# Four half vectors of the conditioning on VectorE from the query groups on, and one on TensorE

## The reference, cut to what matters

```
silu_c = silu(c);  silu_cc = silu(c_ctx)
for l in 0, 1:                                   # 2 layers, 256 tokens, width 2048
    sh_m, sc_m, gt_m, sh_f, sc_f, gt_f = split(silu_c @ w_mod[l] + b_mod[l], 6)
    ux = rmsnorm(x) * g[0] * (1 + sc_m) + sh_m
    if l == 0:
        k_c, v_c = split(modulate(ctx, ..., silu_cc) @ w_in[:, 2048:])
        f, q, k, v = split_even(ux @ w_in)       # 1024, 1024, 256, 256 columns
        attn = window_attention(rope(q), rope(k), v, k_c, v_c, sink)
        mix = concat([fft2 per group(f).real, attn]) @ w_out
    else:
        mix = short_conv_mix(ux, ...)
    x = x + gt_m * rmsnorm(mix)
    x = x + gt_f * rmsnorm(relu(modulate(x, g[2], sh_f, sc_f) @ w1)**2 @ w2)
```

## Time and profile before

| | us |
|---|---|
| median of three runs (2260.5 to 2265.11) | 2263.23 |
| profiled execution | 2260.15 |
| its span, first to last instruction | 2258.4 |
| TensorE busy in it | 2197.8 (97%) |
| VectorE busy | 1653.4 (73%) |
| ScalarE busy | 1019.5 (45%) |

### The profile page before, as it was taken

The page is one execution under the profiler, slowest core; times in us unless marked ns, Lnnn a source line. Parts: engine busy times, 40 slices in busy tenths (PEclk is TensorE's granted clock), DMA queues, the critical chain, the costliest instruction groups (busy, mean ns, idle before and its releaser), DMA issues.

```text
span 2258.4 us, 30977 instructions
## 1 busy us (share of the span) xinstructions
PE 2197.8 (97%) x11355; PEld 1806.4 (80%) x11355; DVE 1653.4 (73%) x1784; ACT 1019.5 (45%) x1269; POOL 97.7 (4%) x32
## 2 busy tenths in 40 slices
PE   6899999999999999999989999999999999999998
PEld 3478568788888888888868888887888888888887
DVE  0266767888788888888988889988888554654665
ACT  3163544554344345344454444446534443443443
POOL 0000000001010010110101101100011000000000
PEclk8899999999999999999999999999999999999999
DMA  9966978688888888889868788896887656666664
GB/s 374 352 224 226 373 273 298 231 295 278 302 275 285 290 272 292 294 275 318 291 213 279 272 298 280 275 310 226 288 286 247 198 193 189 188 193 193 205 195 149
DMA packets 253896, 592.63 MB, mean 262 GB/s; under 512 B 18082, under 2 KB 18610, under 8 KB 253234
## 3 DMA queue, kind: packets, MB, share of 16 engines
q1 hardware_dynamic: 253746, 590.63, 77.6%
HBM read 588.46 MB, written 2.10 MB: 261 GB/s over the span
## 4 chain that ended last, share of the span: by engine, by line
PE 87%; DVE 5%; DMA 4%; issue 2%; ACT 2%; SPq 1%; DVEq 0%; ACTq 0%
PE ps L520 30%; PE ps L526 15%; PE ps L595 11%; PE ps L596 11%; PE ps L597 11%; PE ps L559 2%; DMA early<-in_w_mod_dram 2%; DVE wlo L1276 1%; DMA mraw<-in_w_mod_dram 1%; DMA raw<-in_mlp_w_dram 1%; DVE acc L1286 1%; PE ps L481 1%; ACT whi L908 1%; DMA raw<-in_att_w_out_dram 1%; PE ps L687 0%
## 5 line engine op out<-in xcount | busy, mean ns | idle before, releaser
L1276 DVE TENSOR_TENSOR wlo<-raw,whi 128x1024 fp32r<-128x1024 f32 x712 | 901.0, 1270 | 429.1 <-ACT whi L908 427.7
L908 ACT ACTIVATE whi<-raw 128x1024 fp32r<-128x1024 f32 x712 | 751.7, 1059 | 946.9 <-PE ps L597 384.6
L520 PE MATMUL ps<-u,whi 128*128 128x512 f32 x2944 | 930.1, 397 | 9.8 <-DVE wlo L1276 5.7
L526 PEld LDWEIGHTS ps<-u,wlo 128*128 128x128 f32 x2944 | 555.1, 189 | 131.5
L526 PE MATMUL ps<-u,wlo 128*128 128x256 f32 x2944 | 580.2, 279 | 0.0
L595 PE MATMUL ps<-whi,h 128*128 128x512 f32 x1216 | 474.6, 390 | 6.9 <-DVE wlo L1276 6.8
L597 PE MATMUL ps<-whi,h 128*128 128x512 f32 x1216 | 473.2, 389 | 0.0
L596 PE MATMUL ps<-wlo,h 128*128 128x512 f32 x1216 | 473.2, 389 | 0.0
L520 PEld LDWEIGHTS ps<-u,whi 128*128 128x128 f32 x2944 | 450.2, 189 | 17.1 <-issue 10.8
L1286 DVE SCALAR_TENSOR_TENSOR acc<-mraw,cs,acc 128x1024 f32<-128x1024 f32 x240 | 306.7, 1278 | 3.9 <-DMA mraw<-in_w_mod_dram 3.9
L595 PEld LDWEIGHTS ps<-whi,h 128*128 128x128 f32 x1216 | 228.3, 188 | 57.3 <-DVE wlo L1276 10.2
(11 more groups left out here) (195 smaller groups left out, 1258.3 us busy)
## 6 DMA issues: line engine op xcount, KB each, us to landing
raw<-in_mlp_w_dram SPq DMA_DIRECT2D x512, 512.0 KB, 4.7
mraw<-in_w_mod_dram SPq DMA_DIRECT2D x272, 512.0 KB, 5.4
early<-in_w_mod_dram SPq DMA_DIRECT2D x96, 512.0 KB, 6.7
raw<-in_conv_w_in_dram SPq DMA_DIRECT2D x96, 512.0 KB, 5.2
raw<-in_att_w_in_dram SPq DMA_DIRECT2D x40, 512.0 KB, 4.4
raw<-in_att_w_out_dram SPq DMA_DIRECT2D x32, 512.0 KB, 6.4
raw<-in_conv_w_out_dram SPq DMA_DIRECT2D x32, 512.0 KB, 6.0
raw<-in_w_mod_dram SPq DMA_DIRECT2D x16, 512.0 KB, 7.1
```

Source lines behind the costliest of these rows:

```text
L520: return pe.matmul(ps[:, 4 * slot + m, :], whi[:, s % SLOTS, cols], src[:, k, :], start=(k == 0), stop=False)
L526: return pe.matmul(ps[:, 4 * slot + m, 0:T], wlo[:, s % SLOTS, cols], src[:, k, 0:T], start=False, stop=(k == KC - 1))
L908: act.activation(whi[:, s, :], raw[:, s, :], ACT.Copy).then_inc(hi_ready, 1)
L1276: dve.tensor_tensor(wlo[:, s, :], raw[:, s, :], whi[:, s, :], ALU.subtract).then_inc(lo_ready, 1)
```

## The change

Units 0, 1, 4 and 2, in this order, are summed on VectorE by `mraw`, in the accumulators 1, 0, 1, 0 (`FIRST_UNITS`, `FIRST_ACC`), and unit 3 alone on TensorE. That is 64 unit slabs on VectorE, as against 32 by `mraw` and 16 by `early`, and 16 on TensorE in place of 32; 80 loads in both. The late unit and its loads are gone. `UNITS_BESIDE` says how many unit slabs stand beside each weight slab: 6 beside 8 to 15, 9 beside 16 to 23, 4 each beside 24, 25 and 26, 28 beside 27 to 43 (steps t = 0 to 16) and 9 in steps 17 to 21. SyncE loads slab m+2 four weight slabs further on. TensorE's pairs are at t = 8 to 15. Columns are made for unit 0 ahead of the Fourier steps, unit 1 at t = 4, unit 2 at t = 22, in bank 2, after all 64 unit slabs; one gate is spread at t = 18, the other with output slab 1, after `finish_first(2, 2)`. The accumulator of the first two units is started anew once its columns are done (`columns_done`). The number of `mraw` buffers is the same.

```diff
@@ SyncE
-            for w in range(SL, W_F + 6):
-                att_slab(w)
-                for m in FIRST_LOADS.get(w, ()):
-                    first_unit_slab(m)
-            for t in range(-1, 17):
-                att_slab(W_F + t + 7)
-                ...
-                if t != 1 and t < 16:
-                    mix_pair(t if t > 0 else t + 1)
-                if t >= 0:
-                    first_unit_slab(t + 13)
-            ...
+            for w in range(SL, slab_of(PG_WO) + SL):
                 att_slab(w)
+                for m in units_beside(w - SLOTS):
+                    if m + 2 < len(FIRST_UNITS) * UNIT:
+                        first_unit_slab(m + 2)
+                if w == W_F + 6:
                     sp.wait_ge(slab_used, W_KV + SL)
+                for n in MIX_LOADS.get(w - (W_F + 7), ()):
+                    mix_pair(n)
+            for m in range(units_before(slab_of(PG_WO) + SLOTS) + 2, len(FIRST_UNITS) * UNIT):
+                first_unit_slab(m)
@@ TensorE
+            unit_columns(0, 6)
             for t in range(24):
                 ...
-                if t == 21:
-                    pe.wait_ge(mix_copied, 2)
-                    pe.wait_ge(m_used, UNIT)
+                if t == 4:
+                    unit_columns(1, 6)
+                if t == 18:
+                    pe.wait_ge(mix_copied, 1)
+                    pe.wait_ge(m_used, 3 * UNIT)
+                    spread_gate(ones, acc[:, 1, :], 6)
                 if t == 22:
-                    pe.wait_ge(m_used, DVE_FIRST * UNIT)
-                if t >= 21:
-                    unit_columns(t - 21)
+                    pe.wait_ge(pt_copied, 2 * HEADS)
+                    unit_columns(2, 2)
@@ VectorE
                     lo(SL * (i + 1) + s, s % SLOTS)
-                    for m in FIRST_SLABS[i][s]:
+                    for m in units_beside(SL * (i + 1) + s):
                         first_unit_slab(m)
@@
             for s in range(3):
                 lo(W_F + s, s)
-                first_unit_slab(8 + s)
+                for m in units_beside(W_F + s):
+                    first_unit_slab(m)
@@
-                if t < 21:
-                    first_unit_slab(11 + t)
+                for m in units_beside(W_F + 3 + t):
+                    first_unit_slab(m)
+                if t == 6:
+                    finish_first(0, 6)
+                    finish_first(1, 6)
                 ...
-                for k in LATE_AT.get(t, ()):
-                    late_unit_slab(k)
-            finish_first()
+            finish_first(2, 2)
@@ tables
-FIRST_SLABS = (((), (), (), (), (0,), (), (), (1,)), ((2,), (3,), (4,), (5,), (6,), (), (), (7,)))
+MIX_LOADS = {4: (0,), 6: (1,), 8: (2,), 9: (3,), 10: (4,), 11: (5,), 12: (6,), 13: (7,)}
+UNITS_BESIDE = ((0, 1, 1, 0, 1, 1, 1, 1), (1, 1, 1, 0, 2, 1, 1, 2), (4, 4, 4),
+                (2, 2, 1, 2, 1, 2, 2, 2, 1, 2, 1, 2, 2, 2, 1, 2, 1), (2, 2, 2, 2, 1))
 def mix_slabs(t):
 
-    return range(2 * (t - 2), 2 * (t - 1)) if 2 <= t < 18 else ()
+    return range(2 * (t - 8), 2 * (t - 7)) if 8 <= t < 16 else ()
```

More of the change, by code:

```diff
@@ L98, in first_slab @@
 def first_slab(un):
-    return (un - 3) * UNIT
+    return (un - 1) * UNIT
 def unit_col(u):
@@ L677, in fourier_slab, with mix_slab @@
                 last.then_inc(slab_used, 1)
[L679 to L684, removed]
+            def mix_slab(k):
+                if k == 0:
+                    pe.wait_ge(mod_ready, 2)
+                pe.wait_ge(mix_landed[k % SLOTS], 16 * (k // SLOTS + 1))
                 for half in range(2):
@@ L749, in channel_dft, with unit_columns, spread_gate @@
                 last.then_inc(fb_done, 1)
-            def unit_columns(un):
-                src, pick = ((acc[:, 0, :], ones[:, 0:2]), (acc[:, 1, :], ones[:, 0:2]), (mix_row[0], sel))[un]
+            def unit_columns(un, bank):
+                pe.wait_ge(m_used, (FIRST_UNITS.index(un) + 1) * UNIT)
+                src = acc[:, FIRST_ACC[FIRST_UNITS.index(un)], :]
                 for c in range(KC // 2):
[L755 to L758, removed]
+                    last = pe.matmul(ps[:, bank, 16 * un + 2 * c:16 * un + 2 * c + 2], src[:, c * P:(c + 1) * P],
+                                     ones[:, 0:2], start=True, stop=True)
+                last.then_inc(columns_done, 1)
+            def spread_gate(pick, rows, bank):
+                for n in range(2):
+                    last = pe.matmul(ps[:, bank + n, :], pick, rows[:, n * 512:(n + 1) * 512], start=True, stop=True)
+                last.then_inc(gate_spread, 1)
+            unit_columns(0, 6)
             for t in range(24):
@@ L1289, in first_unit_slab @@
             def first_unit_slab(m):
-                un, k = divmod(m, UNIT)
-                a, src = acc[:, un, :], mraw[:, m % 2, :]
+                n, k = divmod(m, UNIT)
+                a, src = acc[:, FIRST_ACC[n], :], mraw[:, m % 2, :]
                 dve.wait_ge(m_landed[m % 2], 16 * (m // 2 + 1))
@@ L1585, in take_fourier, with finish_first @@
                     dve.tensor_copy(fin[:, a, i * GW:(i + 1) * GW], ps[:, 4 + a, :]).then_inc(sum_done, 1)
-            def finish_first():
-                dve.wait_ge(columns_done, 1)
-                for un in range(3):
-                    col = unit_col(un)
-                    dve.tensor_tensor(vt[:, col:col + KC // 2],
-                                      ps[:, 6, 16 * un:16 * un + 16].rearrange("p (c w) -> p c w", w=2)[:, :, 0],
-                                      bT[:, col:col + KC // 2], ALU.add).then_inc(mod_ready, 1)
+            def finish_first(un, bank):
+                col = unit_col(un)
+                dve.wait_ge(columns_done, un + 1)
+                dve.tensor_tensor(vt[:, col:col + KC // 2],
+                                  ps[:, bank, 16 * un:16 * un + 16].rearrange("p (c w) -> p c w", w=2)[:, :, 0],
+                                  bT[:, col:col + KC // 2], ALU.add).then_inc(mod_ready, 1)
             for t in range(25):
```

86 lines of the change are left out of this document (27 added, 59 removed).

## The result

The changed kernel takes 2291.96 us (median of four runs, 2286.98 to 2297.09) against 2262.22 us before. The recorded ratio is 1.0138, with a 95% interval of 1.0114 to 1.0162 (the two medians alone would give 1.0131): 1.4% slower. The forecast was 2286, slower, within 2268 to 2300.

What follows compares the result with a forecast made beforehand. The prediction took TensorE to bound the kernel before, and VectorE's unit slabs, waiting on two-buffer load turns, to delay it after. Terms +28.2 - 0.8 - 2.2 - 3.4 + 1 = +23 us gave a median of 2286, range 2268 to 2300.

Steps and rivals of the forecast that it cites:

- Price of a unit slab: VectorE's conditioning additions: two buffers give two slabs per 5.3 us turn, 2.65 us each, with loads landing in 4.0 us.
- (a): Second query group: unit slabs 0 and 1 cost nothing, slabs 2 to 4 delay weight slab 15; TensorE loses 2.8 us.
- with (a) hidden: Lower bound: the query group's 2.8 us vanish and loads land in 3.4 us, giving +12, 2275.
- (b): Key/value group: nine unit slabs in place of six, slab 13 starts at about 195.0, TensorE loses nothing.
- (c): First three Fourier slabs: 4, 4 and 4 unit slabs make the key copy 22 us later; TensorE waits 19 us.
- (d): Up to Fourier slab 8: 14 more unit slabs delay VectorE's accumulator copies; TensorE starts that slab 28 us late.
- (e): Fourier slab 8 to output stage: TensorE paces again and saves 2.2, 0.8 and 3.4 us; gate spread 1.9 in and out.
- (f): TensorE's half clock after idle waits: free where it waits for VectorE again, 1 us after the last wait.
- The sum: Whole kernel: +28.2 - 0.8 - 2.2 - 3.4 + 1 = +23 us, so 2283 profiled and 2286 at the median.
- Faster: Rival, chance 0.09: TensorE stays the bound, 8 pairs (8.8 us) and most idle time are gained: 2250.
- The cover is larger: Rival, chance 0.04: delay at Fourier slab 8 is near 6 us and equals what is saved, no difference: 2263.
- Much slower: Rival, chance 0.13: delays add up with low clock after each wait and saturated loads: above 2298, about 2303.

Runs made afterwards that it cites:

- second profile: The changed kernel run once more without edits, with more runs and another profile: 2293.68 us, 1.0144 (1.0127 to 1.0160) against the kernel before.

## Why the prediction was right, step by step

**Price of a unit slab.** Right. Foretold: one turn of 5.3 us for two slabs, 2.65 each, at a landing of 4.0. Measured: 2.55 us each, at a median landing of 3.9. Two, three and four buffers order the time as this says, though with a landing that grows from 3.9 to 5.6 us.

**(a) Query group.** Foretold 2.8 us, measured 3.5 (165.7 against 162.2). TensorE waited four times, 1.11, 0.41, 1.21 and 1.20 us. 0.6 us of the 3.5 are there before slab 2 already, and the step that failed is small: "slabs 0 and 1 fall before 148.94, where VectorE idled 4.55 us: nothing". In the changed kernel:

```profile
140.25 1.28 DVE L1280 SCALAR_TENSOR_TENSOR acc<-mraw,cs,acc 128x1024 f32<-128x1024 f32 x1
143.30 5.13 ACT L994 ACTIVATE y<-y 32x512 f32<-32x512 f32 x8 [2.31 <-DVE y L1470]
149.55 1.22 DVE L1255 TENSOR_TENSOR wlo<-raw,whi 128x1024 fp32r<-128x1024 f32 x1 [4.55 <-ACT whi L887]
```

The idle time is as long as before, and it comes 0.6 us later. It is ScalarE's turn at work that VectorE itself released, so unit slab 1 (140.25), which stands ahead of that release, does not fall into it but moves it, by 1.2 us, of which the low halves before it give back 0.6 by an earlier start (139.11 against 139.70). The 2.8 us that the bounds take off "with (a) hidden" had no ground either: what stalls TensorE here delays VectorE's chain by the same slabs, and with two of them elsewhere the key copy came 2.2 us earlier, too (in one profile).

**(b), (c).** Slab 13 at 197.16 (foretold 195.0), slab 15 at 203.40 (200.5), the key copy at 232.6 (230.4), the scores at 238.1 (235.8). The chain was in the right places, 2 to 3 us late. Of the 2.2 us at slab 13, 0.7 come from (a), 0.2 from slabs 9 and 10, two additions in a row that take 2.6 us and not 2.4, and 1.1 from the load of slab 11, which took 5.1 us to land where the sum had 4.0:

```profile
mraw<-in_w_mod_dram SPq DMA_DIRECT2D x1, 512.0 KB, 5.1
...
188.63 1.29 DVE L1280 SCALAR_TENSOR_TENSOR acc<-mraw,cs,acc 128x1024 f32<-128x1024 f32 x1 [1.46 <-DMA mraw<-in_w_mod_dram]
```

Slab 15 is later again, by 0.7 us: its load was issued at 198.47, with a `raw` load just before it, and took 4.9. From there the 11 slabs took 28.0 us and not the 28.6 of the sum. So the key copy is only 2.2 us late because two errors, slow landings ahead of the turns and slightly quick ones within them, have opposite signs.

**(d).** The copies end at 282.9 (foretold 279.7), and TensorE starts Fourier slab 8 at 283.04, 31.4 us later than before (foretold 28.2). 2.2 of the 3.2 us are those of the key copy. In the second profile it is 285.83.

**(e).** From there to the output stage TensorE took 89.9 us against 94.1. Foretold was 0.8 + 2.2 + 3.4 less and 1.9 more for the spread that moved in, 4.5 us; measured 4.2. The spread should have come back as 1.9 us in the output stage, but that stage took 91.7 us against 92.1: one wait for a low half is 2.0 us long there, against 1.1 before, which is 0.9 of the 1.5 us missing. The whole rest of the span is within 2.5 us of the kernel before in both profiles of the changed kernel.

**(f) Clock.** Right in kind. In the stretch 238 to 260 the mean clock was 0.66:

```profile
238.00:260.00 22.00, 14.53 (x40) 9.56 (x41) 15.90 (x22) 7.02 (x12) 0.00 (x0) 0.66 0.73 240
```

TensorE waits for VectorE again right behind it, so most of this is free, as the prediction had it. The 1 us that the sum has for the low clock after the last wait is not there in the first profile: the clock is 1.00 from 282.90 on. In the second the first products of Fourier slab 8 are at half clock, 0.63 us each.

**The sum.** Foretold +23, measured +26.8 in the profiled executions and +29.7 between the medians. The terms that were too small are (a) to (d), 3.2 us together in the first profile and 6.0 in the second, by the landings above and the 0.7 us of (a). In the first profile 0.3 us of (e) and 1.4 us of what the gate's spread should have given back are missing, too, and the 1 us of (f) goes the other way: 3.2 + 0.3 + 1.4 - 1.0 = 3.9, the difference between the spans' 26.7 and the 22.8 of the sum.

**The rivals.** "Faster" needed a turn under 3.6 us; turns were 5.1 us. "The cover is larger": none was. "Much slower" needed 2298; the slowest single run was 2297.91. The waits on `mraw` (foretold 40 us or more) are 41.6. TensorE's idle time up to the output stage was foretold at 30 to 45 us; it is 25.2 after 211.75 and 3.9 in the query group, 29.1 in all, just under the range. Part of what I had counted as idle was spent in products at half clock, 0.63 us in place of 0.40.

## What to carry to other kernels

Idle time of an engine is room for work only if that work's data arrive at the pace of the idle time. With n buffers the pace is one round trip (use, issue, landing) divided by n, here 5.1 us by two, and neither the engine's busy share nor the transfer rate shows it. Look for it in the rows where an addition waits for its own load although the transfers are below their rate (256 GB/s in 197 to 217, against 384 in the earlier trace rows). When you add buffers, put a longer landing into the sum: 3.9 us with two became 5.2 with three and 5.6 with four.

Ask also who ends the idle time. VectorE's 4.55 us ended with ScalarE's work that VectorE had released, so a slab ahead of the release cost its full time, and one behind it cost nothing. And follow the in-order queue behind the waiting instruction: here it was not the conditioning that was late but the key copy behind it.

## What the runs showed of the hardware that was not expected

Additions of 128 x 1024 numbers that follow each other directly start 1.36 to 1.39 us apart (four in 5.45 us). With other work behind it an addition takes 1.20 (159.15 to 160.34 in the earlier trace rows). The program lets each unit slab wait for the one before it (`m_used`). The shared accumulator is not what it takes: slab 16 goes into the other one and starts 1.39 us behind slab 15 (203.40, 204.79). That the wait on the semaphore makes the difference was not tested.

A load of 512 KB landed in 3.9 us (median) and one of 256 KB in 2.9 in the same place: more than the 0.7 us that the bytes alone would give at the rate of the saturated stretch (384 GB/s). With more buffers, so more loads under way, 512 KB landed in 5.2 us at 305 GB/s and 5.6 at 363. The Trainium skill, DMA: Bandwidth & Descriptors, "Anatomy of one DMA", has about 2.0 us plus bytes over 436 GB/s for another issue path, by estimate 3.2 and 2.6 us; both landings are above that, by 0.7 and 0.3 us.
